# A two-block transformer forward pass on one NeuronCore: four places where instructions change their order

## The reference, cut to what matters

```python
x = x + m @ w_out                       # first block: mixers, then 16 of 16384 experts per head
h2 = rmsnorm(x, g_ffn)
x = rmsnorm(x + peer_ffn(h2, ...), g_final)
# second block, layer 0
xn = rmsnorm_2(h, norm_mix[0])
q, k, v, g, lr, mq = split_cols(xn @ gla_w_in, GLA_SIZES)
log_a = log_sigmoid(lr @ gla_w_gate_up + gla_b_gate) / 16
main = gla_mixer(q, k, v, log_a, g, gla_out_norm)     # decays over all pairs of positions
mo = mem_attention(mq, mem_kv)                         # 4 heads: softmax(q k) v over 256 memory rows
h = h + concatenate([main, mo]) @ w_out[0]
h = h + conv_ffn(rmsnorm_2(h, norm_ffn[0]), ...)
# layer 1: the same with nsa_mixer (12 heads, compressed and windowed softmax) in place of gla_mixer
return rmsnorm_2(h, final_norm)
```

## Time and profile before

| | us |
|---|---|
| median of three runs | 1634.73 (1631.59 to 1637.02) |
| the profiled execution | 1635.63 |
| its span in the trace | 1633.8 |
| TensorE busy / VectorE / ScalarE / GpSimd | 1509.1 / 941.8 / 412.5 / 596.8 |
| TensorE idle, by what ended it: ScalarE in the expert stage | 91.4 in 77 waits |
| the first weights | 7.9 |
| `wout0`'s weights (L2304) | 2.4 |
| ready to issue, before the projection at L1868 | 1.8 |
| VectorE's L1565 before the transposes L2227 | 1.7 in 2 waits |
| VectorE's L1792 before the transposes L2464 | 1.6 |

### The profile page before, as it was taken

The page is one execution under the profiler, slowest core; times in us unless marked ns, Lnnn a source line. Parts: engine busy times, 40 slices in busy tenths (PEclk is TensorE's granted clock), DMA queues, the critical chain, the costliest instruction groups (busy, mean ns, idle before and its releaser), DMA issues. The chain is left out here.

```text
span 1633.8 us, 22069 instructions
## 1 busy us (share of the span) xinstructions
PE 1509.1 (92%) x7680; PEld 1137.3 (70%) x7682; DVE 941.8 (58%) x2401; ACT 412.5 (25%) x1006; POOL 596.8 (37%) x525
## 2 busy tenths in 40 slices
PE   7999899898999877777799999999999999999998
PEld 6999845554455323232357778999999878899997
DVE  5652686666766867666556535555552135555554
ACT  2120232222222222222125422111122145311112
POOL 4850243333433444334333006555510000455551
PEclk9999999999999999999999999999997999999999
DMA  8464799999999999999974118544334310555431
GB/s 335 158 225 158 298 427 426 427 426 427 426 409 426 420 426 428 427 421 415 428 288 135 66 63 332 166 155 157 125 120 128 108 48 1 213 173 167 156 128 39
DMA packets 63383, 420.63 MB, mean 257 GB/s; under 512 B 7340, under 2 KB 7788, under 8 KB 16812
## 3 DMA queue, kind: packets, MB, share of 16 engines
q0 software_dynamic: 38560, 277.19, 40.8%
q1 hardware_dynamic: 24736, 142.35, 25.0%
HBM read 417.28 MB, written 3.45 MB: 258 GB/s over the span
## 5 line engine op out<-in xcount | busy, mean ns | idle before, releaser
L2137 PE MATMUL wide<-arena 128*128 128x512 f32 x1024 | 472.1, 608 | 91.4 <-ACT arena L658 91.4
L2137 PEld LDWEIGHTS wide<-arena 128*128 128x128 f32 x1024 | 189.6, 192 | 351.5 <-issue 193.2
L1418 DVE CUSTOM_DVE_ANT_0 arena<-arena,wide 128x1024 f32<-128x1024 f32 x256 | 312.5, 1221 | 184.8 <-DMA arena<-uv_dram,arena 179.1
L498 POOL DMA_INDIRECT arena<-uv_dram,arena x256 | 259.4, 1013 | 403.4 <-PE wide L2137 286.8
L658 ACT ACTIVATE arena<-arena 128x2 f32<-128x2 f32 (+4 forms) x205 | 72.2, 354 | 527.6 <-DVE arena L1418 409.6
L2377 PE MATMUL wide<-arena,wring 128*128 128x256 f32 x704 | 158.6, 379 | 0.0
L1630 DVE SCALAR_TENSOR_TENSOR arena<-arena,prm 128x255 f32<-128x255 f32 (+1 forms) x152 | 126.0, 849 | 55.6 <-ACT arena L658 55.5
L2377 PEld LDWEIGHTS wide<-arena,wring 128*128 128x128 f32 x704 | 131.0, 190 | 16.1
L1664 DVE TENSOR_TENSOR arena<-bank,arena 128x128 f32<-128x128 f32 x266 | 74.0, 290 | 105.1 <-PE bank L2337 101.6
L509 POOL TENSOR_TENSOR arena<-arena 128x512 f32<-128x512 f32 x15 | 20.2, 1348 | 299.0 <-ACT arena L658 298.3
L658 ACT ACTIVATE arena<-bank 128x128 f32<-128x128 f32 (+8 forms) x101 | 40.3, 401 | 311.2 <-PE bank L2337 104.4
(11 more groups left out here) (296 smaller groups left out, 2139.5 us busy)
## 6 DMA issues: line engine op xcount, KB each, us to landing
wring<-ffn_dram SPq DMA_DIRECT2D x44, 1024.0 KB, 5.1
wring<-ffn_dram SPq DMA_DIRECT2D x44, 512.0 KB, 3.5
wring<-win_dram SPq DMA_DIRECT2D x15, 1024.0 KB, 5.3
wring<-wout_dram SPq DMA_DIRECT2D x12, 1024.0 KB, 4.8
wring<-wq_dram SPq DMA_DIRECT2D x5, 1024.0 KB, 7.1
wring<-mix_dram SPq DMA_DIRECT2D x4, 1024.0 KB, 5.5
arena<-uv_dram,arena POOLq DMA_INDIRECT x256, 11.9
wring<-memkv_dram SPq DMA_DIRECT2D x4, 1024.0 KB, 9.1
```

Of the source, the lines that this page charges most:

```text
L498: pool.indirect_dma_start(out=G[:, n % NBUF, :], out_offset=None, in_=a["uv"], in_offset=bass.IndirectOffsetOnAxis(ap=idx[:, u, r:r + 1], ...
L1418: V.tensor_tensor_reduce(out=G[:, n % NBUF, 0:D], in0=G[:, n % NBUF, 0:D], in1=wide[:, 0:2, :].rearrange("p a b -> p (a b)"), scale=1.0, s ...
L2137: ins = MM(wide[:, 2 + h, :], diag[:, n % 4, e, :], G[:, r % NBUF, D + 512 * h:D + 512 * (h + 1)], start=r % (HEADS * TOPK) == 0, stop=r % ...
```

## The change

Four orders are changed and nothing is added to or taken from the arithmetic: every engine has the same instructions as before. `finish` takes a range of tiles.

```diff
-            def finish(dst, src, col):
-                for k in range(KT):
+            def finish(dst, src, col, ks=range(KT)):
+                for k in ks:
...
-            finish(hT, xT, fin[:, 2, :])
+            finish(hT, xT, fin[:, 2, :], range(0, 2))
             b = full("gla_qk0")
             for m in range(2):
                 V.scalar_tensor_tensor(out=gq[32 * m:32 * m + 32, 3, :], ...)
             V.tensor_tensor(halves(b, DK), halves(b, DK), rstd[0:DK, :]..., ALU.mult).then_inc(scaled0, 1)
+            finish(hT, xT, fin[:, 2, :], range(2, KT))
             norm("mean_fin", xT, [(xT, "g_final", 0)])
...
             probs(0)
+            probs(1)
             decayed(3)
             maxi(2)
             keep_pairs(3)
-            probs(1)
             decayed(4)
             maxi(3)
+            probs(2)
             keep_pairs(4)
-            probs(2)
             decayed(5)
+            probs(3)
             keep_pairs(5)
-            probs(3)
...
-            for J in range(3):
-                nsa_max(J)
+            nsa_max(0)
+            nsa_max(1)
             nsa_probs(0)
+            nsa_max(2)
...
-            for n in range(4):
-                for i in range(4):
-                    wout0(i, n)
             for i in range(4):
-                for n in range(4, KT):
+                for n in range(KT):
                     wout0(i, n)
```

## The result

| | before | after |
|---|---|---|
| median, us (runs) | 1633.34 (1631.59 to 1637.02, 6) | 1618.18 (1613.19 to 1622.99, 6) |
| ratio of the times | | 0.9903 (95%: 0.9874 to 0.9932) |
| the profiled execution | 1635.63 | 1622.99 |
| its span | 1633.8 | 1621.2 |
| mean granted clock | 0.982 | 0.988 |

The changed kernel is faster by 15.2 us of medians, 1.0%, where 11.7 were forecast. The two profiled executions differ by 12.6.

The account below looks back on a forecast made before the run. TensorE, busy 92% of the span, bounds the kernel, so only holes and lower-clock stretches can yield time. Gains 1.8 + 1.7 + 1.3 + 3.8 and clock 3.1 make 11.7: 1635.63 to 1623.9, less 0.9: 1623.0 us, range 1618.0 to 1629.5.

Parts of the forecast that it names:

- The clock behind the holes at A and C: Half-clock losses after two holes: 2.9 us at A, 3.2 at C; middles 1.5 and 1.6 were taken as gain.
- A: Layer 0 start, gate scaling ahead of six norms: 1.83 us hole before `gla_qk1` goes, gain 1.8; clock 1.5 more.
- C: Layer 1 attention, job 0's probabilities earlier: 1.60 us hole before the first turn shrinks, gain 1.3; clock 1.6 more.
- B: Memory heads' probabilities one place earlier: holes of 0.83 and 0.84 us before `turn(1)` and `turn(3)` go, gain 1.7.
- D: `wout0` tile by tile: the wait for the fourth tile's weights goes, gain 3.8 us, 2.4 idle and 1.4 clock.
- Rival 4: Whole kernel: the change does nothing, each place having another bound close behind; 1634.7 us, chance 0.02.
- rival 2: Removed waits at A, B and C are replaced by others, only D's gain remains; 1630.9 us, chance 0.13.
- The tables' lateness: At A, tables sent 1.6 us later delay the gate sums some tenths; 7.3 us of cover protects TensorE.
- The collision with GpSimd: At B, the moved `probs(2)` starts beside GpSimd's L630: up to 1.3 us later, costed at nothing.
- all of A's and C's clock comes back: Case with both half-clock losses, after the holes at A and C, fully regained: 1620.0 us.
- Rival 1: Holes go but the clock stays low at A and C; 1626.1 us, chance 0.17.
- Rival 3: Layer 1 attention, without its hole, falls to the lower clock: 31 us more, 1657 us, chance 0.02.

Follow-up runs that it names:

- x1: Kernel before with only the gate scaling moved ahead of six norms (A); ratio to before 0.9988, stretch A 20.34 us.
- x4: Kernel before with only `wout0` taken tile by tile (D); ratio to before 0.9945, stretch D 27.62 us.
- x5: The changed kernel profiled again, no edit; ratio to before 0.9887.
- x7: Changed kernel with D's hole put back: `wout0` first multiplies one input tile into each of four outputs; ratio to before 0.9918, stretch D 32.16 us.
- x10: The changed kernel profiled a third time, no edit; ratio to before 0.9906.
- x2: Kernel before with only the memory heads' probabilities moved earlier (B); ratio to before 0.9977, stretch B 82.94 us.
- x3: Kernel before with only job 0's probabilities in layer 1's attention moved earlier (C); ratio to before 0.9986, stretch C 98.29 us.
- x6: Changed kernel with the gate scaling (A) put back as before; ratio to before 0.9938, stretch A 24.09 us.
- x8: Changed kernel with the compressed keys' 68-column matmuls mixed with the first query projection (256 columns); ratio to before 0.9887, that stage 60.46 us.
- x9: x8 with job 4's memory-head probabilities, `probs(4)`, also moved earlier on VectorE; ratio to before 0.9908, compressed-key stage 60.24 us.

## Why the direction and the mechanisms held, and which terms of the sum failed

Two steps of the prediction failed.

1. **The clock behind the holes at A and C, halved** ("I take the middle, 1.5", "middle 1.6"). All of it came back: 3.05 and 3.2.
2. **The sizes of B and D.** For B the bracketed idle time, 1.7, was taken as all that the holes cost; it was 2.13. For D the full-clock duration was made from 0.221 per instruction of a short row, a gain of 3.8 with an upper bound of 4.2; it was 4.31.

- **Direction and mechanisms.** All five holes went, each for the reason given, and each part alone (x1 to x4) gives its stretch what it gives in the whole, to 0.25 us. Rival 4 is thus out, and so is rival 2: the only wait of TensorE that came in place is the 0.44 of the second turn at C.
- **A.** The place of the wait, the copy's end and the norms that stay ahead of TensorE came as worked out. The tables' lateness varied by 1.8 us between profiles and was covered, as the prediction had it. The hole gave its 1.83. The clock's 2.9, halved to 1.5, came back whole, 17.03 to 13.98, 3.05. The worry was that the small gate matmuls alone could hold the clock down. In the seven profiles without the hole (after, x1, x5, x7 to x10), all at 20.33 or 20.34, they never did; in the five with it (before, x2, x3, x4, x6) the stretch took 3.75 to 5.04 more, every time.
- **B.** 2.13 where 1.7 were put, and 1.7 was called the upper bound. The two idle times in the trace are 0.83 and 0.84, but the start-to-start times around the two turns shrank by 1.05 and 1.06, which is all of the 2.13. Without a hole a turn starts 0.17 before the end that the trace gives to the matmuls ahead of it (900.78 against 899.89 + 1.06); with a hole this overlap is lost on top of the idle time. At A the same 0.16 stands between 5.04 and 1.83 + 3.05. The collision with GpSimd lengthened the clamp by 1.4 us, 0.1 beyond its bound, and was free, as costed.
- **C.** The hole gave 1.60 - 0.44 = 1.16 of the 1.3. The clock term failed in the same way as A's: halved to 1.6, it came back whole, 4.37 - 1.16 = 3.2, the upper bound. In the four profiles with the hole (before, x1, x2, x4) C took 101.1 to 102.9, in the eight without it 98.3 to 98.5.
- **D.** 4.31 where 3.8 were put and 4.2 was the bound. The full-clock duration of the whole was mis-sized: 28.3 was made from 0.221 per instruction, a row's duration over 32. The rows of 32, 64 and 128 such instructions took 7.07, 13.98 and 27.79, which is 0.216 for each and 0.16 once; the fixed part weighs more in a short row. And no tile waited for its last linear-attention piece.
- **The sum.** A 5.04 for 3.3, B 2.13 for 1.7, C 4.37 for 2.9, D 4.31 for 3.8: 15.85 for 11.7. Three quarters of the shortfall (1.74 and 1.47 of 4.15) are at the two halved clock terms. The case "all of A's and C's clock comes back", 1620.0, was the nearer one: its sum is 14.7, and the 1.1 that is left lies mostly in D and B. Of the 4.8 between 1623.0 and 1618.18, another 1.4 is the median of before, 1633.34 from six runs, where the prediction had 1634.73 from three.
- **What the sum is counted against.** The prediction read one execution of the kernel before, in which all three clock parts had their larger size. In other profiles with the same holes they were smaller: behind A 1.8 (x2, x3, x6), behind C 1.4 (x2), behind D nothing (x1, x2). The one profile of x2 has all three of these, and against it the same four parts are worth 3.75 + 2.13 + 2.58 + 2.40 = 10.9 and not 15.85. So 1.5 and 1.6 are near what some executions lose, by luck: the reason given for halving, that the low clock might stay without the hole, came true in no profile.
- **Rival 1** fell in every profile without the hole. Its argument, that 1237 to 1252 runs at 0.50 with TensorE busy, was true of that stage and did not carry to A and C.
- **Rival 3** did not come: the 13 us from the first turn show 1.00. Its threshold of about 14 us is a slip; 13.5 lost at 0.83 each is 16, as its own bracket says.
- **What the prediction had not seen** is that the stage of the compressed keys, from which rival 1 took its argument, has two speeds. It gave "about 2 us" for half-clock stretches that shift elsewhere. This stage alone moved by 9.4 us between executions of one program, more than any part of the change. That the 15.2 of the medians comes near the local 15.85 is thus largely luck: both kernels have runs in each group, and against x2 the local sum would be 10.9.

What stays open: what decides, in the stage of the compressed keys, which of the two speeds an execution gets. The 16 us ahead of it show 1.00 and a busy TensorE whether the clock falls or not, and the instructions across the fall are the same. Also open is what gives the stretch at half clock behind a hole its different sizes, and the 3 us by which the time up to A varies.

## What to carry to other kernels

In this kernel a hole on TensorE cost its length and, in most profiles, what the clock took behind it: removing 5.4 us of holes at A, C and D gave 13.7, of which 3.05, 3.2 and 1.7 are the clock's. To size such a term, read the slow stretch behind the hole at its full-clock duration and take the whole difference, unless a profile shows the same work slow with no hole ahead; and do it in more than one profile with the holes in it, since here the four parts come to 15.85 against one execution and to 10.9 against another. And judge parts of a few us by the stretch between two fixed instructions, which repeated to 0.02 us here, when a stage elsewhere moves the whole time by 9.

## What the runs showed of the hardware that was not expected

- At the end of a run of 32 matmul instructions of 36 columns, or within 1 us behind it, the clock fell from 1.00 to 0.50 in seven of twelve profiles (before, after, x2, x3, x8, x9, x10), with TensorE busy all the time, and did not fall in the other five. The changed kernel alone did both (after and x10 against x5).
- Once fallen, it stayed at 0.50 for 17 to 20 us in the five profiles in which 64 matmul instructions of 68 columns came next, which took 13.92 us against 7.82 at 1.00. In the two in which these were mixed with matmuls of 256 columns (x8, x9) it was back after some 3 us.
- The same hole in `wout0` (2.39 to 2.46 us) was followed by half clock in three of five profiles (before, x3, x7: D 32.0 to 32.2, its last 116 instructions 26.90 to 26.96) and not in the other two (x1, x2: 30.3 and 25.27). The shorter holes of 1.83 and 1.60 were followed by it in nine of nine: the projection behind the first took 15.74 to 17.03 against 13.98 without the hole (before, x2, x3, x4, x6), the first `wout1` piece behind the second 2.54 to 3.39 against 1.89 (before, x1, x2, x4). So the length of a hole alone does not say whether the clock falls behind it, nor how much is lost: the same 1.83 us hole cost 1.8, 2.9 or 3.05 beside its own length.
- VectorE's clamp of 256 numbers took 1.54 us beside GpSimd's 1.90 us instruction and 0.17 without it. The two ended within 0.03 us of each other (905.50 and 905.47), as in the kernel before, where the clamp took 0.94 (897.99 and 897.97).
